# Eighteen stages on one core: the order of work around each stage boundary, the place of the last products, and the root of the norm

## The chip, the cores and the metric

The kernel runs on one core of one Trainium2 chip, as one program for the whole network. The metric is the device time of that program in microseconds, lower is better. The time before is the median of three runs, 3973.99 us (3971.36 to 3976.38).

## The reference

The input is one sequence of 256 tokens of 1024 features (tile 0 and tile 1 are its two halves of 128 tokens). Eighteen sublayers follow each other, and each has this form:

```
h = x * rsqrt(mean(x*x) + 1e-6) * gain           # (in stages 6 to 17 also * (1 + scale) + shift)
x = x + gate * sublayer(h)                       # gate only in stages 6 to 17, else 1
glu sublayer:  (silu(h @ w_gate) * (h @ w_up)) @ w_down
```

The kernel numbers them: 0 nsa attention, 1 moe, 2 ple, 3 moba attention, 4 moe, 5 ple, then 6 ffn, 7 rwkv, 8 ffn, 9 ffn, 10 mamba, 11 ffn, 12 ffn, 13 swa attention, 14 ffn, 15 ffn, 16 rwkv, 17 ffn. A moe stage computes all 32 experts and weighs them by the router. A ple stage multiplies a sigmoid of one product with another product. An ffn stage has 22 units of 128 hidden features, a moe stage 32.

## The kernel before

Each product of fp32 matrices is made of three: every weight piece of 128x1024 is split by ScalarE into a rounded high part (`split_hi`) and by VectorE, or for some pieces by GpSimd, into the rest (`split_lo_v`, `split_lo_g`), and the same holds for the activations. `mm3_tokens` issues the three matmuls (high x low, high x high, low x high). The split pieces live in eight slots; a piece can be split only once its slot's former piece has been used for the last time (`product["used", ...]`) and once its chunk has landed from DRAM in a ring of 12 units. Which slot a piece takes is written by hand, in the lists at the calls of `ffn`, `moe`, `ple` and in `swa` and `mamba`. Each engine follows a program in a fixed order, so that an instruction that waits holds back all that stand behind it on its engine. SyncE issues the weight chunks in order, and between them the gate rows (`load_gate`).

A glu stage (`plan_glu`, `glu_pe`, `glu_act`, `glu_dve`) goes over pairs of units. Step s = 2p + t is pair p for tile t: `gate_up(s)` is 24 matmuls of 512 columns, `silu(s)` and `up(s)` make the hidden features, `turn(s)` transposes them on TensorE, `high(s)` and `low(s)` split them, and `down(s, hf)` adds them (6 matmuls) to half hf of tile t's output. The steps overlap: `turn(s - 1)` stands inside `gate_up(s)` and the down products of step s - 2 behind it. `second(p)` plans the two pieces of the down weights of pair p.

A boundary is what lies between two stages. The output of tile t, half hf is added to x by `update(t, hf)` on VectorE (in stages 6 to 17 one scalar_tensor_tensor that multiplies by the gate row, line 238, then one add, line 226). Then the norm: `square_act` sums the squares on ScalarE, `var_dve` makes mean and half, `root_act` a first root by Ln and Exp on ScalarE (its table set loaded by `e.tables`, line 268), `root_dve` one Newton step and the scaling of half of the row (`unit_act` scales the other half), `pe` transposes the tile on TensorE, and `halves_act` and `halves_dve` apply gain and shift and split the result. TensorE's first product of the next stage waits for that (`x_lo`). `early(st + 1)` are the next stage's first weight pieces, which are split in this stretch too. In a glu stage tile 1 of the head is transposed by `second_tokens`, after k = 4 of the eight k of `gate_up(0)`. A mixer stage (attention, rwkv, mamba) transposes tile 1 before any product, because its products take both tiles.

The gate row of a stage is written from SBUF to DRAM and read back on all partitions; in the row that is read back, feature k*128 + p stands at p*8 + k, so that `gated_dve` reads it with a step of 8 elements.

## Time and profile before

| | |
|---|---|
| median of 3 runs | 3973.99 us |
| profiled execution, its own time | 3970.69 us |
| its span | 3968.9 us |
| TensorE busy | 3645.8 us (92%) |
| VectorE busy | 2628.6 us (66%) |
| ScalarE busy | 1798.6 us (45%) |
| GpSimd busy | 429.9 us (11%) |
| mean granted TensorE clock | 0.96 |

The span holds the instructions; the rest of the execution's own time, 1.8 us, lies around them. TensorE is idle for 323 us of the span. Each boundary can be seen in the timeline as a stretch of a few microseconds in which TensorE's rows carry an idle time in brackets, with the engine and line that ended it.

### The profile page before, as it was taken

How to read it: one execution, taken by the hardware profiler on the slowest of the kernel's cores; microseconds unless marked ns; L12 is line 12 of the kernel's file. 1: busy time of each engine (PE TensorE's matmuls, PEld its weight loads, DVE VectorE, ACT ScalarE, POOL GpSimd, SP SyncE). 2: the span in 40 equal slices, each digit the busy share in tenths (PEclk: the TensorE clock that was granted, in tenths of full speed). 3: DMA queues.
4: the chain of work that ended last, by engine and by line, in shares of the span. 5: the costliest groups of instructions: out<-in, count | busy, mean ns of one | idle time of the engine just before them, and what ended most of it. 6: DMA issues, size and time to landing. Idle time of an engine off the chain costs nothing.

```text
span 3968.9 us, 51736 instructions
## 1 busy us (share of the span) xinstructions
PE 3645.8 (92%) x19842; PEld 2996.3 (75%) x19842; DVE 2628.6 (66%) x4865; ACT 1798.6 (45%) x3151; POOL 429.9 (11%) x365
## 2 busy tenths in 40 slices
PE   6999998899898989889998998999989998899899
PEld 6767877688687867778787957878768787777677
DVE  4567765677576665577777677777667777665555
ACT  3254444544544433354546545454454544433343
POOL 2010002100001322200003410000000002322100
PEclk9899998999899999999999999999999999999999
DMA  5126852377485310167673416867347674300153
GB/s 229 54 81 244 281 196 81 122 282 282 144 292 212 108 43 1 38 218 285 224 276 128 165 65 220 294 226 272 122 139 288 221 290 154 117 12 1 59 181 106
DMA packets 170898, 670.13 MB, mean 169 GB/s; under 512 B 20512, under 2 KB 21024, under 8 KB 162464
## 3 DMA queue, kind: packets, MB, share of 16 engines
q1 hardware_dynamic: 170656, 666.83, 47.0%
q8 instruction: 160, 2.62, 0.3%
q14 instruction: 82, 0.67, 0.1%
HBM read 665.66 MB, written 1.10 MB: 168 GB/s over the span
## 4 chain that ended last, share of the span: by engine, by line
PE 77%; DVE 14%; ACT 7%; issue 2%; POOL 1%; DMA 0%; SPq 0%; DVEq 0%; ACTq 0%; POOLq 0%
PE pb L273 72%; PE pb L280 4%; ACT wp L264 2%; DVE wp L226 2%; DVE wk L238 2%; DVE wk L226 2%; DVE sq L238 1%; DVE pb L238 1%; ACT wk L264 1%; DVE xt L226 1%; ACT hT L264 1%; ACT sq L264 1%; ACT hx L264 1%; DVE hx L226 1%; ACT L264 1%
## 5 line engine op out<-in xcount | busy, mean ns | idle before, releaser
L273 PE MATMUL pb<-wp,hx 128*128 128x512 f32 (+1 forms) x6432 | 1587.7, 399 | 32.0 <-DVE hx L226 30.1
L226 DVE TENSOR_TENSOR wp<-ring,wp 128x1024 fp32r<-128x1024 f32 (+1 forms) x903 | 1057.9, 1205 | 608.1 <-ACT wp L264 607.3
L273 PEld LDWEIGHTS pb<-wp,hx 128*128 128x128 f32 x6432 | 1208.1, 192 | 283.9 <-DVE hx L226 22.6
L264 ACT ACTIVATE wp<-ring 128x1024 fp32r<-128x1024 f32 x936 | 957.7, 1053 | 401.4 <-PE pb L273 390.6
L273 PE MATMUL pb<-wp,ex 128*128 128x512 f32 x2928 | 702.0, 389 | 0.0
L273 PEld LDWEIGHTS pb<-wp,ex 128*128 128x128 f32 x2928 | 548.9, 188 | 113.6
L264 ACT ACTIVATE wk<-pb 128x256 f32<-128x256 f32 (+4 forms) x604 | 262.2, 439 | 624.5 <-PE pb L273 450.1
L226 POOL TENSOR_TENSOR wp<-ring,wp 128x512 fp32r<-128x512 f32 (+1 forms) x123 | 235.5, 1919 | 2692.6 <-ACT wp L264 2692.6
L273 PE MATMUL pb<-wk 128*128 128x128 f32 (+8 forms) x3008 | 388.5, 293 | 21.6 <-ACT wk L264 6.6
L273 PEld LDWEIGHTS pb<-wk 128*128 128x128 f32 (+4 forms) x3008 | 286.8, 172 | 115.1 <-issue 45.2
L273 PE MATMUL pb<-hx,wp 128*128 128x256 f32 x2688 | 344.3, 288 | 22.6 <-DVE hx L226 12.0
L273 PEld LDWEIGHTS pb<-hx,wp 128*128 128x128 f32 x2688 | 333.5, 195 | 30.7 <-issue 21.3
L243 DVE CUSTOM_DVE_ANT_0 ring<-ring,cact,prm 128x1024 f32<-128x1024 f32 x288 | 354.2, 1278 | 0.0
L264 ACT ACTIVATE ex<-pb 128x256 fp32r<-128x256 f32 x240 | 92.1, 385 | 514.9 <-PE pb L280 514.9
L280 PE MATMUL pb<-cst,wk 128*128 128x128 f32 (+2 forms) x1092 | 197.1, 284 | 64.6 <-DVE wk L226 48.5
L280 PEld LDWEIGHTS pb<-cst,wk 128*128 128x128 f32 (+2 forms) x1092 | 133.0, 142 | 125.0 <-DVE wk L226 56.6
L264 ACT ACTIVATE wk<-wk 128x256 f32<-128x256 f32 (+3 forms) x305 | 127.1, 435 | 185.7 <-DVE wk L238 65.6
L226 DVE TENSOR_TENSOR wk<-wk,pb 128x256 f32<-128x256 f32 (+1 forms) x256 | 117.5, 459 | 114.6 <-ACT wk L264 73.3
L280 PE MATMUL pb<-cst,sq 128*128 128x128 f32 x352 | 61.3, 326 | 135.0 <-DVE sq L232 128.1
L280 PEld LDWEIGHTS pb<-cst,sq 128*128 128x128 f32 x352 | 48.1, 167 | 149.2 <-issue 118.6
L226 DVE TENSOR_TENSOR ex<-pb,ex 128x256 fp32r<-128x256 f32 x240 | 100.7, 420 | 78.6 <-ACT ex L264 76.9
L226 DVE TENSOR_TENSOR wk<-pb,cst 128x256 f32<-128x256 f32 (+3 forms) x212 | 80.4, 429 | 73.5 <-PE pb L273 62.4
(176 smaller groups left out, 2767.7 us busy)
## 6 DMA issues: line engine op xcount, KB each, us to landing
ring<-weights SPq DMA_DIRECT2D x1088, 512.0 KB, 5.1
ring<-weights SPq DMA_DIRECT2D x35, 1536.0 KB, 6.5
ring<-weights SPq DMA_DIRECT2D x24, 1024.0 KB, 5.1
cst<-gate_rows SPq DMA_DIRECT2D x12, 512.0 KB, 4.3
cst<-consts SPq DMA_DIRECT2D x1, 1984.0 KB, 10.7
ring<-weights SPq DMA_DIRECT2D x1, 1280.0 KB, 5.4
ring<-weights SPq DMA_DIRECT2D x1, 1152.0 KB, 5.5
xt<-x_in SPq DMA_DIRECT2D x1, 1024.0 KB, 5.0
```

What stands on the lines that cost most here:

```text
L226: return self.real.tensor_tensor(out, a, b, op) if self.real else Uncounted()
L238: return self.real.scalar_tensor_tensor(out=out, in0=a, scalar=s, in1=b, op0=op0, op1=op1)
L243: return self.real.tensor_tensor_reduce(out=out, in0=a, in1=b, scale=1.0, scalar=first, op0=op0, op1=op1, accum_out=accum)
L264: return self.real.activation(out, a, func, bias=bias, scale=scale, accum_out=accum)
L273: return self.real.matmul(out, l, r, start=start, stop=stop, skip_group_check=skip)
L280: return self.real.transpose(out, a, self.identity[base:base + n, base:base + n])
```

## The change

1. **Root.** `root_act` goes, and with it the table load at the boundary. `var_dve` makes a first guess from the bits of the variance and `root_dve` takes three Newton steps, ten small VectorE instructions in all, each waiting for the one before.
2. **Gate row.** It is written to DRAM in the order of the features, element by element, and read with step 1 by `gated_dve`.
3. **Boundary.** The early pieces are now split one at a time between the other steps: one before the squares, one between them (VectorE: before `var_dve`), one before `halves`, the rest before tile 1's norm. Out of a glu stage VectorE does `halves_dve(0)` before `update(1, 0)`; the last step's `up` and `low` stand behind `var_dve(0)` and `root_dve(0)`, and its `silu` and `high` behind tile 0's squares.
4. **Last products.** The down weights of the last pair are split a step earlier, in slots that are free by then. Tile 0's last down products stand after k = 2 of the last `gate_up`, and the last four products are all tile 1's.
5. **Glu start.** Tile 1's head is transposed after k = 7, not 4. In ffn stages `turn(0)` stands after k = 5 of `gate_up(1)`, not 1.
6. **Slots.** Eight of the hand-written lists change.

```
@@ -745,8 +745,7 @@
...
             x, ps = X2[:, t, hf * 512:(hf + 1) * 512], pb[2 * t + hf][:, :]
-            p3 = ps.rearrange("p (k n) -> p k n", k=4)
-            e.stt(p3, p3, scale, gate_rows[:, hf * 4:(hf + 1) * 4, :], ALU.mult, ALU.mult).then_inc(
+            e.stt(ps, ps, scale, gate_row[:, hf * 512:(hf + 1) * 512], ALU.mult, ALU.mult).then_inc(
                 *v_step.up((st, "gated", t, hf)))
@@ -782,27 +781,24 @@
...
             e.wait_ge(*a_step[self.st, "square", t, 1])
-            v = self.column(t, 2)
-            e.ts(v, self.column(t, 0), self.column(t, 1), 1.0 / D, ALU.add, ALU.mult).then_inc(
-                *v_step.up((self.st, "var", t)))
-            e.wait_ge(*v_step[self.st, "var", t])
-            e.ts(self.column(t, 3), v, 1e-6, -0.5, ALU.add, ALU.mult).then_inc(*v_step.up((self.st, "half", t)))
-
-        def root_act(self, e, t):
-            e.wait_ge(*v_step["eps"])
-            e.wait_ge(*v_step[self.st, "var", t])
-            e.act(self.column(t, 4), self.column(t, 2), ACT.Ln, bias=eps[:, 0:1]).then_inc(*a_step.up((self.st, "log", t)))
-            e.wait_ge(*a_step[self.st, "log", t])
-            e.act(self.column(t, 5), self.column(t, 4), ACT.Exp, scale=-0.5).then_inc(*a_step.up((self.st, "root", t)))
+            v, h, y = self.column(t, 2), self.column(t, 3), self.column(t, 4)
+            e.ts(v, self.column(t, 0), self.column(t, 1), 1.0 / D, ALU.add, ALU.mult).then_inc(*v_step.up())
+            e.wait_ge(*v_step.last)
+            e.ts(h, v, 1e-6, -0.5, ALU.add, ALU.mult).then_inc(*v_step.up())
+            e.wait_ge(*v_step.last)
+            e.ts(v, h, -2.0, None, ALU.mult).then_inc(*v_step.up())
+            e.wait_ge(*v_step.last)
+            e.ts(y.bitcast(I32), v.bitcast(I32), -0.5, RSQRT_MAGIC, ALU.mult, ALU.add).then_inc(*v_step.up((self.st, "first", t)))
 
         def root_dve(self, e, t):
-            r = self.column(t, 5)
-            e.wait_ge(*a_step[self.st, "root", t])
-            e.wait_ge(*v_step[self.st, "half", t])
-            e.stt(self.column(t, 6), r, r, self.column(t, 3), ALU.mult, ALU.mult).then_inc(*v_step.up((self.st, "newton", t)))
-            e.wait_ge(*v_step[self.st, "newton", t])
-            e.ts(self.column(t, 7), self.column(t, 6), 1.5, r, ALU.add, ALU.mult).then_inc(*v_step.up((self.st, "r", t)))
-            e.wait_ge(*v_step[self.st, "r", t])
+            h, z = self.column(t, 3), self.column(t, 6)
+            e.wait_ge(*v_step[self.st, "first", t])
+            for y, r in ((4, 5), (5, 4), (4, 7)):
+                e.stt(z, self.column(t, y), self.column(t, y), h, ALU.mult, ALU.mult).then_inc(*v_step.up())
+                e.wait_ge(*v_step.last)
+                e.ts(self.column(t, r), z, 1.5, self.column(t, y), ALU.add, ALU.mult).then_inc(
+                    *v_step.up(*([(self.st, "r", t)] if r == 7 else [])))
+                e.wait_ge(*v_step.last)
             e.ts(XS[:, t, 0:512], X2[:, t, 0:512], self.column(t, 7), None, ALU.mult).then_inc(
@@ -893,49 +887,59 @@
...
 
-    def boundary_act(e, st, pieces=None, middle=()):
+    def boundary_act(e, st, first=None, then=None, middle=()):
         h, now = head_of(st + 1), early(st + 1)
-        split_hi(e, now[:2] if pieces is None else pieces)
+        split_hi(e, now[:2] if first is None else first)
+        then = now[2:] if then is None else then
+        if h is None:
+            for step in middle:
+                step()
+            return
+        h.square_act(e, 0, 0)
+        split_hi(e, then[:1])
+        h.square_act(e, 0, 1)
         for step in middle:
             step()
-        if h is None:
-            return
-        e.tables("natural_log_exp_and_others")
-        split_hi(e, now[2:3])
-        h.square_act(e, 0, 0)
-        split_hi(e, now[3:])
-        h.square_act(e, 0, 1)
-        h.root_act(e, 0)
         h.unit_act(e, 0)
-        h.square_act(e, 1, 0)
+        split_hi(e, then[1:2])
         h.halves_act(e, 0)
-        h.square_act(e, 1, 1)
-        h.root_act(e, 1)
+        split_hi(e, then[2:])
+        for hf in range(2):
+            h.square_act(e, 1, hf)
         h.unit_act(e, 1)
...
 
-    def boundary_dve(e, st, update, order, pieces=None, middle=()):
+    def boundary_dve(e, st, update, order, first=None, then=None, middle=()):
         h, now = head_of(st + 1), early(st + 1)
-        split_lo_v(e, now[:2] if pieces is None else pieces)
-        if h is not None:
-            h.gains_dve(e)
+        split_lo_v(e, now[:2] if first is None else first)
+        then = now[2:] if then is None else then
         before = order[:order.index((0, 1))]
...
             update(t, hf)
-        for step in middle:
-            step()
+        if h is not None:
+            h.gains_dve(e)
         update(0, 1)
         if h is not None:
-            split_lo_v(e, now[2:3])
+            split_lo_v(e, then[:1])
             h.var_dve(e, 0)
+            for step in middle[:1]:
+                step()
             h.root_dve(e, 0)
+            for step in middle[1:]:
+                step()
+            split_lo_v(e, then[1:2])
+        else:
+            for step in middle:
+                step()
+        if h is not None and middle:
+            h.halves_dve(e, 0)
         if (1, 0) not in before:
             update(1, 0)
-        if h is not None:
+        if h is not None and not middle:
             h.halves_dve(e, 0)
-            split_lo_v(e, now[3:])
         update(1, 1)
         if h is not None:
+            split_lo_v(e, then[2:])
             h.var_dve(e, 1)
@@ -1043,7 +1047,7 @@
...
         def second(p, by="v"):
-            at = [order[(4 * p + j) % 6 if p == P - 1 else 6 + j] for j in range(2)]
+            at = [order[(4 * P + j) % 6 if p == P - 1 else 6 + j] for j in range(2)]
             g.down.append([made(lambda I, j=j: unit(I, p)[1][:, j * 1024:(j + 1) * 1024], at[j], by) for j in range(2)])
@@ -1059,11 +1063,11 @@
...
             a = second(p - 1, by) if p and not late else []
-            b = gate_up(p + 1, 0, 2) if more else []
+            b = gate_up(p + 1, 0, 2) if more else second(p)
             g.split.append(a + b)
...
                 g.ada[2 * p + 1] = plan_ada()
-            a = second(p - 1) if late else second(p) if not more else []
+            a = second(p - 1) if late else []
             b = gate_up(p + 1, 2, 4, "g" if routed and p == 0 else "v") if more else []
@@ -1126,7 +1130,7 @@
...
 
-        second_tokens = {4: lambda: head.pe(e, 1)}
+        second_tokens = {7: lambda: head.pe(e, 1)}
         if g.routed:
@@ -1142,17 +1146,16 @@
...
             gate_up(0, second_tokens)
-            gate_up(1, {1: lambda: turn(0)})
+            gate_up(1, {5: lambda: turn(0)})
         for s in range(6 if g.routed else 2, last):
...
             whole_down(s - 2)
-        gate_up(last, {1: lambda: turn(last - 1)})
-        down(last - 1, 0)
+        turn(last - 1)
+        gate_up(last, {2: lambda: whole_down(last - 1)})
+        down(last - 2, 0)
         turn(last)
-        down(last - 1, 1)
-        for hf in range(2):
-            down(last - 2, hf)
-            down(last, hf)
+        down(last - 2, 1)
+        whole_down(last)
         boundary_pe(e, st)
@@ -1188,18 +1191,22 @@
...
             silu(5)
-        for s in range(6 if g.routed else 0, last + 1):
+        for s in range(6 if g.routed else 0, last):
             here = 1 if s % 2 == 0 and s else 0
...
             split_hi(e, g.split[s][here:])
-            if s == last - 1:
-                split_hi(e, early(st + 1)[:2])
             if g.ada.get(s) is not None:
...
             silu(s)
-        boundary_act(e, st, (), [lambda: high(last)])
+        high(last - 1)
+
+        def last_unit():
+            silu(last)
+            high(last)
+
+        boundary_act(e, st, early(st + 1)[:1], early(st + 1)[1:], [last_unit])
@@ -1255,17 +1262,17 @@
...
             modulations(5)
-        for s in range(6 if g.routed else 0, last + 1):
+        for s in range(6 if g.routed else 0, last):
             modulations(s)
...
             split_lo_v(e, g.split[s][here:])
-            if s == last - 1:
-                split_lo_v(e, early(st + 1)[:2])
             up(s)
-        boundary_dve(e, st, update, IN_TURN, (), [lambda: low(last)])
+        modulations(last)
+        low(last - 1)
+        boundary_dve(e, st, update, IN_TURN, early(st + 1)[:1], early(st + 1)[1:], [lambda: up(last), lambda: low(last)])
@@ -1781,7 +1788,7 @@
...
         W = lambda a, b: (lambda I: np.asarray(I["sw_w_qkv_2"])[0][:, a:b])
-        A = grouped(st, range(3, 8), W(1024, 1536), W(0, 1024), in_hx, "h", in_hx, "h", 3072,
+        A = grouped(st, (5, 6, 7, 3, 4), W(1024, 1536), W(0, 1024), in_hx, "h", in_hx, "h", 3072,
                     lambda I: np.asarray(I["sw_w_o_2"])[0], range(3, 8), 3, ("sw_q", "sw_k"), lambda h: C("swa"),
@@ -2045,7 +2052,7 @@
...
         c_dt = raw_chunk(128, 256, lambda I: ktiles(W(6144, 6176)(I)), (v_step, (st, "dt weights")))
-        w = Weights(st, [4, 5, 6, 7] * 8 + [4, 5] * 8, None,
+        w = Weights(st, [6, 7, 4, 5] * 8 + [4, 5] * 8, None,
                     (4096, D, lambda I, n0, n1: W(2048 + n0, 2048 + n1)(I)), (2048, D, lambda I, n0, n1: W(n0, n1)(I)),
@@ -3039,21 +3046,21 @@
...
     moe(1, 0, [0, 1, 2, 3, 4, 5, 6, 7], (x_lo, (0, "o", 7)))
-    ple(2, 0, [4, 5, 6, 7, 2, 3, 0, 1])
+    ple(2, 0, [0, 1, 2, 3, 6, 7, 4, 5])
     moba(3)
     moe(4, 1, [0, 1, 5, 4, 2, 3, 6, 7], (x_lo, (3, "o", 7)))
-    ple(5, 1, [2, 3, 5, 4, 6, 7, 0, 1])
-    ffn(6, 0, 0, 0, [5, 4, 6, 7, 0, 1, 2, 3])
+    ple(5, 1, [0, 1, 5, 4, 6, 7, 2, 3, 5, 4])
+    ffn(6, 0, 0, 0, [0, 1, 2, 3, 6, 7, 5, 4])
     rwkv(7, 0, 0)
-    ffn(8, 0, 2, 1, [4, 5, 6, 7, 3, 0, 1, 2], {i: (product, (7, "out", 1, 1)) for i in range(3)})
+    ffn(8, 0, 2, 1, [4, 5, 3, 0, 6, 7, 1, 2], {i: (product, (7, "out", 1, 1)) for i in range(3)})
     ffn(9, 1, 0, 0, [6, 7, 4, 5, 1, 2, 3, 0])
...
                                                 for i in range(8)})
-    ffn(12, 2, 0, 0, [5, 6, 3, 4, 1, 2, 7, 0])
+    ffn(12, 2, 0, 0, [7, 0, 3, 4, 5, 6, 1, 2])
     swa(13, 2)
-    ffn(14, 2, 2, 1, [6, 7, 0, 2, 1, 3, 4, 5], (x_lo, (13, "o", 7)))
-    ffn(15, 3, 0, 0, [0, 2, 6, 7, 4, 5, 1, 3])
+    ffn(14, 2, 2, 1, [1, 2, 6, 7, 0, 3, 4, 5], (x_lo, (13, "o", 7)))
+    ffn(15, 3, 0, 0, [0, 3, 1, 2, 6, 7, 4, 5])
     rwkv(16, 3, 1)
@@ -3115,7 +3122,7 @@
...
             a = l * 72 + s * 24 + 16
-            e.dma(d_gate[n].rearrange("(p k) -> p k", p=128), mods[:, a:a + 8]).then_inc(s_gate, 16)
+            e.dma(d_gate[n].rearrange("(k p) -> p k", p=128), mods[:, a:a + 8], True).then_inc(s_gate, 16)
             e.wait_ge(s_gate, 32 * n + 16)
```

Besides, `dma` takes the argument `by_element`, `first_head_act` loses its table load and `root_act`, and `Head` takes an argument that nothing reads.

## Rows read from the trace of the kernel before

**Rows 1.** Page, part 1: busy time, share of the span, instructions of each engine

```profile
PE 3645.8 (92%) x19842; PEld 2996.3 (75%) x19842; DVE 2628.6 (66%) x4865; ACT 1798.6 (45%) x3151; POOL 429.9 (11%) x365
```

**Rows 2.** Waits of TensorE, whole span: total us, times, longest us

```profile
PE pb L280 <- DVE sq L232: 128.1, 22, 24.0
```

**Rows 3.** Timeline, stage 14 to 15: start us, us, instruction, [idle before]

```profile
3120.91 7.07 PE L273 MATMUL pb<-wp,ex 128*128 128x512 f32 x30
...
3128.11 1.06 PE L280 MATMUL pb<-cst,sq 128*128 128x128 f32 x8
...
3132.10 5.30 PE L273 MATMUL pb<-wp,hx 128*128 128x512 f32 x15 [2.93 <-DVE hx L226]
...
3139.47 1.06 PE L280 MATMUL pb<-cst,sq 128*128 128x128 f32 x8 [2.06 <-DVE sq L232]
...
3141.86 0.41 DVE L226 TENSOR_TENSOR hx<-hT,hx 128x256 fp32r<-128x256 f32 x1
...
3145.07 1.28 ACT L264 ACT_TABLE_LOAD   x1
...
3147.26 0.69 PE L280 MATMUL pb<-cst,wk 128*128 128x128 f32 x2 [3.25 <-DVE wk L226]
```

**Rows 4.** Windows, stages 14 to 15 (two), 13 to 14; 0.57, 0.50: granted clock

```profile
3132.00:3136.00 4.00, 3.90 (x10) 3.09 (x11) 3.28 (x6) 1.31 (x4) 0.00 (x0) 0.57 0.01 2
3147.00:3152.00 5.00, 4.74 (x12) 3.79 (x13) 5.00 (x9) 2.39 (x3) 0.00 (x0) 0.50 0.92 288
2930.00:2937.00 7.00, 5.12 (x16) 4.07 (x16) 5.15 (x11) 3.48 (x10) 0.00 (x0) 0.50 0.12 40
```

**Rows 5.** Timeline, stage 14 to 15, the norm of tile 1 on VectorE

```profile
3137.52 0.40 DVE L233 TENSOR_SCALAR stat<-stat 128x1 f32<-128x1 f32 x2 [0.79 <-ACT sq L264]
...
3138.59 0.21 DVE L233 TENSOR_SCALAR stat<-stat 128x1 f32<-128x1 f32 x1
3138.84 0.49 DVE L232 TENSOR_SCALAR sq<-xt,stat 128x512 f32<-128x512 f32 x1
```

**Rows 6.** Groups by shape, VectorE, whole span: busy us, mean ns, idle before

```profile
L238 DVE SCALAR_TENSOR_TENSOR pb<-pb,cst 128x512 f32<-128x512 f32 x48 | 53.7, 1120 | 4.7 <-PE pb L273 4.7
L226 DVE TENSOR_TENSOR xt<-xt,pb 128x512 f32<-128x512 f32 x64 | 43.7, 686 | 11.5 <-PE pb L273 9.9
L238 DVE SCALAR_TENSOR_TENSOR wk<-wk,prm,pb 128x256 f32<-128x256 f32 x64 | 28.6, 477 | 8.9 <-PE pb L273 8.9
```

**Rows 7.** Timeline, mixer to ffn: into stage 14 (two rows), into 11

```profile
2920.12 1.23 DVE L226 TENSOR_TENSOR wp<-ring,wp 128x1024 fp32r<-128x1024 f32 x1 [5.57 <-ACT wp L264]
...
2929.83 1.94 PE L280 MATMUL pb<-cst,sq 128*128 128x128 f32 x8 [6.76 <-DVE sq L232]
...
2400.93 1.11 PE L280 MATMUL pb<-cst,sq 128*128 128x128 f32 x8 [4.17 <-DVE sq L232]
```

**Rows 8.** Timeline, ffn to mixer: into stage 7 (two rows), 10, 16

```profile
1272.39 1.06 ACT L264 ACTIVATE wp<-ring 128x1024 fp32r<-128x1024 f32 x1 [5.14 <-PE pb L273]
...
1284.59 1.94 PE L280 MATMUL pb<-cst,sq 128*128 128x128 f32 x8 [5.84 <-DVE sq L232]
...
2111.77 1.94 PE L280 MATMUL pb<-cst,sq 128*128 128x128 f32 x8 [9.09 <-DVE sq L232]
...
3335.42 1.94 PE L280 MATMUL pb<-cst,sq 128*128 128x128 f32 x8 [6.22 <-DVE sq L232]
```

**Rows 9.** Timeline, stage 1 to 2 (moe to ple, two rows), and start of stage 1

```profile
564.73 1.27 PE L280 MATMUL pb<-cst,sq 128*128 128x128 f32 x8 [3.89 <-DVE sq L232]
...
569.04 7.23 PE L273 MATMUL pb<-wp,hx 128*128 128x512 f32 x24 [3.04 <-DVE hx L226]
...
310.17 1.08 PE L280 MATMUL pb<-cst,wk 128*128 128x128 f32 x4 [5.57 <-DVE wk L232]
```

**Rows 10.** DMA issues: count, KB each, median us from issue to landing

```profile
ring<-weights SPq DMA_DIRECT2D x1088, 512.0 KB, 5.1
...
gate_rows<-mods SPq DMA_DIRECT2D x12, 4.0 KB, 5.4
```

More of the change, by code:

```diff
@@ L280, in tp, with dma @@
         return self.real.transpose(out, a, self.identity[base:base + n, base:base + n])
-    def dma(self, out, a):
-        return self.real.dma_start(out, a) if self.real else Uncounted()
+    def dma(self, out, a, by_element=False):
+        return self.real.dma_start(out, a, allow_slow_non_contiguous=by_element) if self.real else Uncounted()
 class Chunk:
@@ L734, in added_dve @@
         return update
-    gates, gate_rows = [], gate_row.rearrange("q (p k) -> q k p", k=8)
+    gates = []
     def plan_gate(st, l, s):
@@ L756, in build_program, with __init__ @@
     class Head:
-        def __init__(self, st, outs, ada=None):
-            self.st, self.outs, self.ada = st, outs, ada
+        def __init__(self, st, outs, ada=None, gated_units=False):
+            self.st, self.outs, self.ada, self.gated_units = st, outs, ada, gated_units
         def gain(self, n, k):
@@ L884, in first_head_act @@
                 h.square_act(e, t, hf)
-            h.root_act(e, t)
             h.unit_act(e, t)
@@ L894, in first_head_dve @@
             h.halves_dve(e, t)
-    def boundary_act(e, st, pieces=None, middle=()):
+    def boundary_act(e, st, first=None, then=None, middle=()):
         h, now = head_of(st + 1), early(st + 1)
-        split_hi(e, now[:2] if pieces is None else pieces)
+        split_hi(e, now[:2] if first is None else first)
[7 more added lines that the diff above has]
+        h.square_act(e, 0, 1)
         for step in middle:
             step()
-        if h is None:
-            return
-        e.tables("natural_log_exp_and_others")
-        split_hi(e, now[2:3])
-        h.square_act(e, 0, 0)
-        split_hi(e, now[3:])
-        h.square_act(e, 0, 1)
-        h.root_act(e, 0)
         h.unit_act(e, 0)
-        h.square_act(e, 1, 0)
+        split_hi(e, then[1:2])
         h.halves_act(e, 0)
-        h.square_act(e, 1, 1)
-        h.root_act(e, 1)
+        split_hi(e, then[2:])
+        for hf in range(2):
+            h.square_act(e, 1, hf)
         h.unit_act(e, 1)
         h.halves_act(e, 1)
-    def boundary_dve(e, st, update, order, pieces=None, middle=()):
+    def boundary_dve(e, st, update, order, first=None, then=None, middle=()):
         h, now = head_of(st + 1), early(st + 1)
-        split_lo_v(e, now[:2] if pieces is None else pieces)
-        if h is not None:
-            h.gains_dve(e)
+        split_lo_v(e, now[:2] if first is None else first)
+        then = now[2:] if then is None else then
         before = order[:order.index((0, 1))]
@@ L1917, in ffn @@
         S = stage(st)
-        S.head = Head(st, [("h", None, Hh, Hl)], (l, s))
+        S.head = Head(st, [("h", None, Hh, Hl)], (l, s), True)
         def unit(I, p):
```

## The prediction

> **What bounds the kernel now.** The page's first part comes first: TensorE is busy for 3645.8 of 3968.9 us [rows 1], so only its 323 us of idle time and its slow stretches can be won or lost. The waits of TensorE say where they lie: 128.1 us, the largest item, end when VectorE has scaled a row for the transposes of the norm [rows 2]. That is a boundary matter, so the timeline of each kind of boundary is read next, and one of the three from ffn to ffn stands in full [rows 3]: TensorE waits 2.93 us between tile 0's transposes and the first product, 2.06 us for tile 1's transposes and 3.25 us at `turn(0)`, 8.24 us together. The windows add what such gaps cost afterwards: behind the first gap TensorE was granted 0.57 of its clock and did 10 products in 3.90 us busy, behind the third 0.50 and 12 in 4.74 us [rows 4]; at full clock (0.50 is 1.2 of 2.4 GHz) 30 products take 7.07 us [rows 3], 0.236 us each, so 10 and 12 would be 2.4 and 2.8 us. The half clock cost 1.5 and 1.9 us, 3.4 us a boundary.
>
> **Unit prices.** *Norm.* Tile 1's norm now takes from 3137.52 to 3138.84, 1.3 us, Ln and Exp included; two VectorE steps that wait for each other are 0.25 us apart [rows 5]. Ten such steps are 2.5 us: the new root is 1.2 us longer, once a tile. The bits step is not in these rows; it is taken as one more of them. *Update.* The gate multiply takes 1.12 us, an add of the same width 0.69, a multiply of that form at half the width, step 1, 0.48 [rows 6]. So step 1 lies between 0.69 and 1.12 us; taken is 0.75, nearer to the row of the same width (twice 0.48 is 0.95). An update falls from 1.8 to 1.4 us. *Halves.* From the transposes' start to the end of the first split pair is 2.8 us with VectorE and ScalarE free [rows 3], so 1.75 us idle behind the 1.06 us of transposes; three more subtractions of 0.41 end the tile at about 4.1. *Piece.* 1.06 us on ScalarE [rows 8], then 1.23 on VectorE [rows 7]. *Table load.* 1.28 us on ScalarE [rows 3].
>
> **Ffn to ffn (3 boundaries).** After tile 0's last product TensorE now has 15 + 6 + 6 + 12 = 39 products instead of 24, 9.2 us instead of 5.7: the transposes of tile 0 don't wait. But `low(last)` stands behind the root. From that product VectorE needs about 0.7 us (rest of the first update, gains), 1.4 (update), 1.2 (piece), 1.0 (four steps), 0.4 (`up`), 1.5 (six steps), 0.5 (scaling), 0.4 (`low`) = 7.1, and TensorE asks after 27 products, 6.4: 0.6 us idle. Then 1.75 idle. `gate_up(0)` follows whole, 5.7 us; from the start of the transposes TensorE is through at 1.06 + 1.75 + 5.7 = 8.5. VectorE: 4.1 (halves) + 2.8 (both updates of tile 1, now behind them) + 1.2 (piece, over the squares) + 2.5 + 0.5 = 11.1. So 2.6 us idle, and now 1.75 behind tile 1's transposes too, which nine products covered. `turn(0)` comes 18 products into `gate_up(1)`, 2.8 + 4.2 = 7.0 us after those transposes; VectorE has halves 4.1, two pieces and `up` done at about 8.1: 1.1 us idle. The sum is 0.6 + 1.75 + 2.6 + 1.75 + 1.1 = 7.8 us for 8.24. With only one half-clock stretch left of two (1.5 us; the gaps are shorter, the two around tile 1's transposes are together longest) it is 9.3 for 11.6: **-2.3 each, -6.9**. The missing table load before `silu(0)` gives only 0.3 us of this, as the two pieces on VectorE end last. The Trainium skill (ScalarE: Activation LUTs, What ACT_TABLE_LOAD costs) puts a switch at 2.66 us, drain included; the trace has 1.28 and no such pause. By the page the saving would be 1.6 us, these three -3.9 more.
>
> **Mixer to ffn.** Into stage 14 the first pieces are held 5.57 us by slots 6 and 7 of the stage's own out-weights, and the updates stand behind them; TensorE waits 6.76 [rows 7]. In slots 1 and 2 nothing holds them: two updates are done before tile 0's last product, and behind it 1.4 + 1.2 + 2.5 + 0.6 = 5.7 us lie beside 24 products. So 6.8 is gone; a piece that now stands before the halves costs 1.2, tile 1 1.4 more, `turn(0)` 1.8 less (1.4 for 3.2): -6.0, and of 4.0 us of half clock (5.12 us busy at 0.50 [rows 4], half of it, and the stretch at `turn(0)`) 1.5 stays: **-8.5**. Into 8 and 17 the same hold remains (slots 4 and 5 stay first): three updates save 1.1, the root takes 1.2, the piece 0.4, tile 1 1.1, `turn(0)` gives 1.9 and its clock 1.5: **-1.8 each**. Into 11 no piece holds (4.17 us [rows 7]), one update saves 0.4: +0.8, +1.2, +0.9, -1.9, -1.5 and a little of the clock: **-1.0**. Together -13.1.
>
> **Mixer to moe (2).** Tile 0 is +0.9 (the piece). Router logits of tile 1 come 2.9 us later, being behind all of `gate_up(0)` and the transposes; all of the choice is on VectorE and TensorE already waits 5.57 us for its end [rows 9]. With `silu(0)` behind the later halves **+3.8 each, +7.6**.
>
> **Ffn to mixer (4).** Both tiles are wanted before a product. Into 10 and 13: 9.09 us idle [rows 8]; `low` +0.6, updates of tile 1 -0.8, `update(1, 0)` no longer beside the transposes +0.3, the root +1.2: **+1.2 each**. Into 16 VectorE has no split to do, so `update(1, 0)` was wholly hidden and is not now: 6.22 us [rows 8] become 8.7, **+2.5**. Into 7 the same, but there ScalarE's third piece waited 5.14 us for a slot [rows 8] and the new list frees it: **-2.6**. Together +2.3. In the mixers the first Exp or Ln now needs a table load; where TensorE runs behind, it is at no cost, if bare 1.28 x 4 = 5 us.
>
> **Moe to ple (2).** Into 2: 3.89 us [rows 9] were a held slot too, now 0.7; 3.04 and 2.8 stay near 2.9 (ple waits for the whole tile); 24 products took 7.23 us for 5.7: **-4.7**. Into 5 no hold: **+0.4**. **Ple onward (2).** Into 3 the root twice, +2.4; into 6 +1.2 + 0.4 + 0.8 - 1.9 = +0.5: **+2.9**. **The end.** Two shorter updates: **-0.7**.
>
> **Gate rows (12).** 128 runs of 32 bytes become 1024 of 4. The trace has 5.4 us to landing [rows 10] and SyncE waits for it. Between nothing and eightfold (43 us) I take the low end, since 512 KB in long runs land in 5.1 us [rows 10]: the 5.4 are hardly a matter of size. Cover: the ring's 12 units; a pair of an ffn uses 9 units in 72 products, 17 us, so 22 us of work are ahead.
>
> **Sum.** -6.9 - 13.1 + 7.6 + 2.3 - 4.3 + 2.9 - 0.7 = -12.2 us on the profiled execution's 3970.7, 3958.5. The median of the runs lies 3.3 us above that execution: **3962 us**.
>
> **Rivals.** (1) *The clock stays up.* The long gaps are cut, and no half-clock stretch is left in the nine glu starts where I keep 1.5 us: -13, 3949. For it: the 2.06 us gap has none behind it [rows 3]; against: 2.6 + 1.75 around 1.06 busy. (2) *The gate multiply is no cheaper.* Then two updates of 0.37 a boundary on the path come back in 12 stages, +9: 3971. Against it: both rows with step 1 [rows 6]. (3) *`turn(0)` waits as before,* since `silu(0)` and `up(0)` stand behind halves that are later: +1.9 in nine stages, 17: 3979. (4) *Slower: a piece in the norm's chain.* Before, one piece stood ahead of tile 0's norm; now VectorE has a piece ahead of each of `var_dve(0)`, `halves_dve(0)` and tile 1's norm, and each waits for ScalarE's copy, which waits for a slot or a chunk. If one is late by its own 1.06 + 1.23 = 2.3 us at all 17 boundaries: +39, 4001. For it: 5.57 and 5.14 us of such holds; against: the new lists follow the order in which slots come free. It decides from 1.2 us a boundary (20 us). (5) *Slower: the element-wise gate rows.* At 43 us to landing, 21 us beyond the ring's cover, 12 times: +250, 4210; it decides from 24 us. The Trainium skill speaks for it (DMA: Bandwidth & Descriptors, Rules for kernel authors): a strided last dimension becomes one descriptor per element, and should be rearranged. No row here shows a transfer of that form.
>
> **Chances.** Forecast 0.38 (own range 3952 to 3971), rival 1 0.20, 2 0.10, 3 0.12, 4 0.14, 5 0.06. 0.2% is 8 us, about what a measurement of this kernel can tell: faster is below 3966. The forecast gives 0.30 to faster and 0.08 to same, rival 1 0.20 to faster, rival 2 0.03 and 0.07, rival 3 same, 4 and 5 slower: 0.53, 0.27, 0.20. The range reaches from rival 1's side, 3940, to half of rival 4, 3988.
>
> **What the profile after would show.** No wait before tile 0's transposes out of ffn stages and into 14; about 0.6 us before the last down products; ten steps on `stat`, 2.5 us, in place of 1.3; the gate multiply at 0.75 us; 2.6 us before tile 1's transposes and 1.75 behind; about 1.1 to 1.4 at `turn(0)`; moe's 5.57 near 9; no more than a few us more to the gate row's landing. Wrong would make it: many more or fewer half-clock stretches, or ScalarE copies that wait for TensorE between the steps of the norm.

## The result, and the profile after

The changed kernel takes 3983.28 us, median of 20 runs (3974.58 to 3989.84), the kernel before in runs beside it 3976.25 (3968.33 to 3980.76). The ratio is 1.0019, 95% interval 1.0012 to 1.0025: slower by 7.5 us, where -12 us was forecast. It lies in the range, on the other side of no change.

Part 1 of the page, as [rows 1]:

```profile
PE 3661.6 (92%) x19842; PEld 3006.9 (75%) x19842; DVE 2637.7 (66%) x5081; ACT 1758.3 (44%) x3061; POOL 431.2 (11%) x365
```

The span is 3987.2 us, so TensorE is idle for 325.6 us, 2.5 more than before. It is busy 15.8 us longer, with as many instructions: the same products ran slower. From here on *half-clock work* is the time in which TensorE was busy while it was granted 0.5 of its clock, summed over the trace: 220.5 us before, 247.4 after. Half of it is time lost: between the two profiles of the changed kernel that stand below it differs by 21.5 us and TensorE's busy time by 12.0. The largest wait fell as it should, and another grew (waits of TensorE, as [rows 2]; the `hx` wait was 45.4 us in 20 times before):

```profile
PE pb L280 <- DVE sq L232: 116.8, 15, 25.0
PE pb L273 <- DVE hx L226: 62.7, 30, 4.0
```

TensorE's timeline from stage 14 to 15 stands against [rows 3]:

```profile
3141.93 3.04 PE L273 MATMUL pb<-wp,ex 128*128 128x512 f32 x12 [0.20 <-DVE ex L226]
3144.81 1.03 PE L280 MATMUL pb<-cst,sq 128*128 128x128 f32 x8
3147.72 7.32 PE L273 MATMUL pb<-wp,hx 128*128 128x512 f32 x24 [1.88 <-DVE hx L226]
3155.65 1.07 PE L280 MATMUL pb<-cst,sq 128*128 128x128 f32 x8 [0.61 <-DVE sq L232]
3158.51 5.94 PE L273 MATMUL pb<-wp,hx 128*128 128x512 f32 x18 [1.79 <-DVE hx L226]
3164.28 0.38 PE L280 MATMUL pb<-cst,wk 128*128 128x128 f32 x2
...
3169.71 0.41 PE L280 MATMUL pb<-cst,wk 128*128 128x128 f32 x2 [2.29 <-DVE wk L226]
```

The last products and tile 0's transposes go through almost without a wait, as planned. Then 24 products take 7.32 us where 5.7 is full clock, and 18 take 5.94 for 4.24: two slow stretches, not one. `turn(0)` (3164.28) no longer waits, but `turn(1)` (3169.71) does, 2.29 us. In the kernel before it did not:

```profile
3155.58 0.38 PE L280 MATMUL pb<-cst,wk 128*128 128x128 f32 x2
```

What VectorE does meanwhile (same stretch; `mods` is the modulations of the first pair, lines between them left out):

```profile
3160.31 2.36 DVE L226 TENSOR_TENSOR wp<-ring,wp 128x1024 fp32r<-128x1024 f32 x2 [0.47 <-ACT wp L264]
3162.59 0.42 DVE L226 TENSOR_TENSOR wk<-wk,pb 128x256 f32<-128x256 f32 x1
3162.92 1.28 DVE L243 CUSTOM_DVE_ANT_0 ring<-ring,cact,prm 128x1024 f32<-128x1024 f32 x1
...
3166.54 0.42 DVE L226 TENSOR_TENSOR ex<-pb,ex 128x256 fp32r<-128x256 f32 x1
3166.88 2.35 DVE L226 TENSOR_TENSOR wp<-ring,wp 128x1024 fp32r<-128x1024 f32 x2
3169.14 0.42 DVE L226 TENSOR_TENSOR wk<-wk,pb 128x256 f32<-128x256 f32 x1
```

Two pieces, `up(0)`, three modulations of 1.28 us, `low(0)`, two pieces and `up(1)` stand in one queue with no gap behind its first piece: `turn(1)` waits for its end. The gate multiply, as [rows 6], takes 0.695 us:

```profile
L238 DVE SCALAR_TENSOR_TENSOR pb<-pb,cst 128x512 f32<-128x512 f32 x48 | 33.4, 695 | 17.7 <-PE pb L273 17.7
```

And the gate row's issues, as [rows 10]:

```profile
gate_rows<-mods SPq DMA_DIRECT2D x12, 4.0 KB, 10.4
```

### The profile page after: what moved, and what is told of

It reads as the page before. It is cut to its first block, busy times and chain, and to the rows that moved or that the text cites. A ratio compares the mean times of both kernels' runs of the same rounds, so it can differ in the third digit from the quotient of the medians.

```text
span 3987.2 us, 51832 instructions
## 1 busy us (share of the span) xinstructions
PE 3661.6 (92%) x19842; PEld 3006.9 (75%) x19842; DVE 2637.7 (66%) x5081; ACT 1758.3 (44%) x3061; POOL 431.2 (11%) x365
## 2 busy tenths in 40 slices
DMA packets 181650, 670.13 MB, mean 168 GB/s; under 512 B 31264, under 2 KB 31776, under 8 KB 173216
## 4 chain that ended last, share of the span: by engine, by line
PE 77%; DVE 14%; ACT 6%; issue 2%; POOL 1%; DMA 0%; SPq 0%; DVEq 0%; ACTq 0%; POOLq 0%
PE pb L273 73%; PE pb L280 4%; DVE wp L226 3%; ACT wp L264 3%; DVE wk L238 2%; DVE wk L226 2%; DVE sq L238 1%; ACT wk L264 1%; DVE stat L233 1%; ACT hT L264 1%; ACT hx L264 1%; DVE ring L243 1%; DVE xt L226 1%; DVE hx L226 1%; DVE sq L226 1%
## 5 line engine op out<-in xcount | busy, mean ns | idle before, releaser
L273 PE MATMUL pb<-hx,wp 128*128 128x256 f32 x2688 | 341.7, 288 | 21.9 <-DVE hx L226 12.1
```

The lines of the kernel that those rows point to most:

```text
L273: return self.real.matmul(out, l, r, start=start, stop=stop, skip_group_check=skip)
```

## The experiments

All ratios are to the kernel before, run on the same chip; 0.001 is 4 us. *Idle* is TensorE's, and it and *half-clock work* are of one profiled execution each. In the kernels with `fill` in their name and in e_last TensorE has added products, which count as busy, so their idle time can't be compared with the others'.

| kernel | ratio (95%) | idle us | half-clock work us |
|---|---|---|---|
| before, two profiles | 1 | 323.1, 322.5 | 220.5, 228.0 |
| changed, two profiles | 1.0019 (1.0012 to 1.0025) | 325.6, 325.1 | 247.4, 225.9 |
| a_root | 1.0065 (1.0052 to 1.0079) | 349.7 | 225.4 |
| a_gate | 0.9961 (0.9948 to 0.9973) | 311.3 | 221.9 |
| a_order | 0.9968 (0.9956 to 0.9981) | 312.9 | 234.9 |
| a_start | 1.0026 (1.0017 to 1.0035) | 323.7 | 248.9 |
| b_root | 0.9988 (0.9979 to 0.9997) | 311.1 | 242.7 |
| b_start | 1.0002 (0.9993 to 1.0011) | 316.8 | 229.4 |
| b_tile1 | 1.0006 (0.9997 to 1.0015) | 319.4 | 236.8 |
| c_best | 0.9957 (0.9945 to 0.9970) | 308.2 | 231.2 |
| d_fill_after | 1.0018 (1.0009 to 1.0027) | 304.8 | 206.9 |
| d_fill_best | 0.9919 (0.9905 to 0.9932) | 271.2 | 181.5 |
| e_mod_before | 0.9994 (0.9984 to 1.0003) | 317.9 | 230.0 |
| e_mod_after | 0.9985 (0.9975 to 0.9994) | 317.9 | 224.9 |
| e_mod_fill_after | 0.9957 (0.9940 to 0.9974) | 292.2 | 183.0 |
| e_mod_fill_best | 0.9919 (0.9903 to 0.9934) | 268.8 | 184.3 |
| e_mod_start | 0.9989 (0.9980 to 0.9997) | 314.6 | 241.9 |
| e_last | 0.9917 (0.9903 to 0.9931) | 274.7 | 188.8 |

### One part alone, on the kernel before

**a_root**: `var_dve` and `root_dve` of the change, no `root_act`, no table load at the boundary.

> The kernel before with one part of the change: the norm's root by VectorE alone (ten dependent steps, no Ln and Exp, no table load at the boundary). Theory A (the root costs what was priced, 1.2 us more a tile, on the path for tile 1 at all 17 boundaries and for tile 0 at about nine, with up to 1.3 us back at turn(0) in eleven glu starts): +15 to +30 us, ratio 1.004 to 1.0075. Theory B (the removed table loads and ScalarE steps give the same back, and the loss comes from the order of the glu starts): within 5 us, ratio 0.999 to 1.0013.

Measured 1.0065, +26 us: theory A. The timeline of its boundary into stage 3, where both tiles are wanted before a product, has 10.11 and 10.17 us where the kernel before has 9.10 and 9.03. Tile 1, here and then in the kernel before:

```profile
628.66 1.97 PE L280 MATMUL pb<-cst,sq 128*128 128x128 f32 x8 [10.17 <-DVE sq L232]
```

```profile
622.09 1.97 PE L280 MATMUL pb<-cst,sq 128*128 128x128 f32 x8 [9.03 <-DVE sq L232]
```

That is 1.0 and 1.1 us a tile. In the whole kernel it is idle time: +26.6 us. The table load it saves gives little: from tile 1's transposes to `turn(0)` into stage 15 are 7.4 us here, 7.8 before.

**a_gate**: the gate row by element, read with step 1.

```
-            e.stt(p3, p3, scale, gate_rows[:, hf * 4:(hf + 1) * 4, :], ALU.mult, ALU.mult)
+            e.stt(ps, ps, scale, gate_row[:, hf * 512:(hf + 1) * 512], ALU.mult, ALU.mult)
```

> The kernel before with one part of the change: the gate row stored by element so that the gate multiply reads it with step 1. Theory A (the multiply falls from 1.12 to 0.69 us, and about two such multiplies a boundary lie on the path in 12 stages): -8 to -12 us, ratio 0.997 to 0.998. Theory B (what the shorter multiply gives is taken back by a later landing of the gate row or by slower work behind the gaps): within 3 us, ratio 0.9993 to 1.0007.

Measured 0.9961, -15.5 us: theory A, and a little more than its 8 to 12 us. Idle time fell by 11.8 us. The row's first transfer takes 11.1 us to land in this run for 5.4 before. SyncE waits longer for it, 127.6 us in 12 times for 60.1; none of TensorE's or VectorE's waits ends with it.

**a_order**: the boundary's order, the last products and the slot lists; root, gate row and starts as before. The old root comes back into the new order like this (one place of the edit to the changed kernel):

```
         for step in middle:
             step()
+        e.tables("natural_log_exp_and_others")
         h.root_act(e, 0)
         h.unit_act(e, 0)
```

> The kernel before with the boundary's order, the slot lists and the last products of the change, and nothing else of it (root, gate row and glu starts as before; the root stands behind the last silu and high, and needs its tables loaded once more there). Theory A (this part gains what the idle time shows: the held pieces into 2, 7 and 14 are gone, 3.8 + 2.6 + 6.8 us, and nothing is lost elsewhere): -10 to -20 us, ratio 0.995 to 0.9975. Theory B (what it saves comes back in other places: more half clock, ex and hx waited for in the last step and behind the pieces): within 6 us, ratio 0.9985 to 1.0015.

Measured 0.9968, -12.7 us, idle -10.2: theory A in size. Its "nothing is lost elsewhere" does not hold: from stage 9 to 10 this part alone has 3.1 us more idle time (see *Held pieces* below). (The lists can't be tried without the order: the early pieces of the old order would wait for slots that come free only behind them.)

**a_start**: the starts alone.

```
-        second_tokens = {4: lambda: head.pe(e, 1)}
+        second_tokens = {7: lambda: head.pe(e, 1)}
-            gate_up(1, {1: lambda: turn(0)})
+            gate_up(1, {5: lambda: turn(0)})
```

> The kernel before with the two glu starts of the change alone: tile 1's transposes behind all of gate_up(0), turn(0) after five blocks of gate_up(1). Theory A (the starts lose by themselves what the first undo gave, 6.5 us: nothing covers the wait behind tile 1's transposes, 1.75 us in eleven starts, less the 1.4 us that turn(0) saves): +4 to +12 us, ratio 1.001 to 1.003. Theory B (they lose only behind the slower root and the later tile 1 of the changed kernel): -6 to +2 us, ratio 0.9985 to 1.0005.

Measured 1.0026, +10.3 us: theory A's size, but not its reason. The idle time is nearly the same, 323.7 us; half-clock work is up 28 us in this profile (21 us above the second one of the kernel before). Into stage 15 of this kernel:

```profile
3160.62 4.40 PE L273 MATMUL pb<-wp,hx 128*128 128x512 f32 x18 [1.79 <-DVE hx L226]
...
3172.19 0.41 PE L280 MATMUL pb<-cst,wk 128*128 128x128 f32 x2 [3.45 <-DVE wk L226]
```

Here the 18 products ran at full clock, and the time went into a wait of 3.45 us at `turn(1)`. So TensorE is early or slow, and `turn(1)` comes at the same time either way, counted from tile 1's transposes: 14.4 us here, 14.1 in the changed kernel.

The four parts alone sum to +25.8 - 15.5 - 12.7 + 10.3 = +7.9 us, against 7.5 for the whole change. That they meet so well is luck, as the next runs show: together the two losing parts cost less than 36.1 us, and the two winning ones give less than 28.2.

### One part taken back in the changed kernel

> The changed kernel with the root as before: Ln and Exp on ScalarE behind a table load, in glu stages behind the last silu and high, and low(last) ahead of the root on VectorE. Theory A (the root is the loss): -15 to -30 us against the changed kernel outside the ffn-to-ffn boundaries, where the second table load takes 1 to 3 us back: ratio to before 0.994 to 0.998. Theory B (the starts are the loss): the table loads (1.28 us each, twice a boundary) come back onto the path as the ten steps leave it, within 5 us of the changed kernel, ratio 1.0005 to 1.003.

> The changed kernel with its glu starts put back: tile 1's transposes after four of the eight feature blocks of gate_up(0) and turn(0) after one of gate_up(1). Theory A (the root is the loss): the idle time only changes places, within 3 us of the changed kernel's 3983, ratio to before 1.001 to 1.0027. Theory B (the starts are the loss, because the first 24 products run together at half clock and nothing covers the wait behind tile 1's transposes): 10 to 20 us faster than the changed kernel, ratio 0.9968 to 0.9994, with 20 us or more of TensorE's 247 us of half-clock work gone.

> The changed kernel with one of the two glu starts put back: tile 1's transposes after four blocks of gate_up(0), turn(0) stays after five of gate_up(1). Theory A (the place of tile 1's transposes is the loss, and turn(0)'s move a gain of up to 1.4 us a start): faster than with both put back, ratio 0.998 to 1.000. Theory B (turn(0)'s move is a loss too, or nothing): ratio 1.000 to 1.001, the same as with both put back or slower.

**b_root** measured 0.9988: the new root costs 12 us there, half of its 26 alone. One reason may be that the old root needs its tables a second time behind the last `silu` in that order; no run tests it by itself. Theory A had the direction, not the size. **b_start** measured 1.0002, 7 us less than the changed kernel: theory B's direction, below its size. **b_tile1**, 1.0006, can't be told from it: the place of tile 1's transposes is most of the starts' loss there, and no gain from `turn(0)`'s move is seen.

> Order, slot lists, last products and gate row of the change, with the root and the glu starts as before: both parts that lost by themselves are left out. Theory A (the parts add up: gate row -14, order and slots -9 as the changed kernel has them): about -20 us, ratio 0.994 to 0.996. Theory B (the second table load in each glu stage, and the order, take back what the gate row gives): -6 to -12 us, ratio 0.997 to 0.9985, and the gate row alone (0.9961) stays the fastest.

**c_best** measured 0.9957, -17 us, inside theory A's range; but the parts don't add up as it says: alone they give 15.5 and 12.7 us. It is not below the gate row alone (0.9961) by more than can be told.

### Is the loss the clock?

Products on constants, as the kernel has them elsewhere, fill the waits of the starts (`repeated_pe`, computing nothing that is used). They stand in the eight ffn starts; the expectations count nine, but the ple stages do not run this code:

```
             ps = bk.hold(e, 4 + s % 3, key, (v_out, key))
+            repeated_pe(e, ps, ahead)
```

> The changed kernel with ten short products on constants (0.156 us each in its profile, 1.6 us) put into the 1.9 us that TensorE waits behind tile 0's transposes and ten into the wait behind tile 1's, in the nine ffn and ple starts. They compute nothing that is used. Theory A (the waits of the starts are what makes the clock fall, and the half-clock work behind them is what the change lost): the half-clock work of TensorE falls by 20 us or more of 247, 8 to 20 us faster than the changed kernel, ratio to before 0.997 to 1.000. Theory B (the half clock comes from elsewhere or by chance): within 4 us of the changed kernel, ratio 1.001 to 1.003.

> Order, slots, last products and gate row of the change with the root and starts of the kernel before, and besides ten short products on constants behind tile 0's transposes and sixteen (2.5 of 3.3 us) before turn(0) in the nine ffn and ple starts. Theory A (the clock follows the waits): -8 to -20 us against the same kernel without them (0.9957), ratio 0.991 to 0.994. Theory B (the clock isn't theirs to keep): ratio 0.995 to 0.997.

> The changed kernel once more, for a second profile. Theory A (the 27 us more of half-clock work are the change's own): half-clock work again 240 to 255 us. Theory B (a good part is chance of one execution, as its 3987 us span lies 4 us above the median): half-clock work 225 to 240 us and a span near 3980.

> The kernel before once more, for a second profile. Theory A: half-clock work again 215 to 225 us, span within 3 us of 3972. Theory B (chance): 225 to 240 us, span above 3973.

**d_fill_best** measured 0.9919, 15 us below c_best: theory A. **d_fill_after** measured 1.0018: nothing, although half-clock work fell by 19 us or more. Ten of the added products take 2.4 us in the trace, not 1.6 as its expectation has it, and what follows them starts 0.1 to 0.2 us later. That is 2 to 3 us in eight starts, too little to explain the missing gain. Its trace into stage 15:

```profile
3151.19 1.07 PE L280 MATMUL pb<-cst,sq 128*128 128x128 f32 x8 [1.14 <-DVE sq L232]
...
3154.25 4.35 PE L273 MATMUL pb<-wp,hx 128*128 128x512 f32 x18
...
3165.24 0.41 PE L280 MATMUL pb<-cst,wk 128*128 128x128 f32 x2 [3.43 <-DVE wk L226]
```

The products behind both waits now run at full clock, and `turn(1)` waits 3.43 us instead of 2.29. From tile 0's transposes to `turn(1)` are 24.9 us in both kernels. The clock was not what bounded this stretch.

**after_2** and **before_2** show what a profile can tell. At equal idle time (325.6 and 325.1) the changed kernel's spans are 3987.2 and 3974.7 us, half-clock work 247.4 and 225.9, most of the difference in stages 1 and 4. So the 27 us between the first two profiles were in good part chance; the means, 236.7 and 224.3, differ by 12.4 us, 6.2 us of time. Both half-clock figures lie in theory B's range (chance); the spans do not follow it, 3974.7 us lying 5 us below its 3980 and 3970.6 in theory A's range. Idle time hardly varies and the medians differ by 7 us, so of the loss some 2.5 us are idle time and the rest, 4.5 to 5 us, is slower work.

### Is it VectorE?

The modulations of the first pair (3.8 us of VectorE) move from step 1 to step 10 of each ffn stage. Seven stages have them in step 1, not eight as the expectation says: in stage 17 none are left.

```
+            if not routed and P > 6 and p == 5:
+                g.ada[2 * p] = plan_ada()
...
-            if (p < 10) if not routed else (2 <= p <= 14):
+            if ((0 if P <= 6 else 1) <= p < 10) if not routed else (2 <= p <= 14):
```

> The changed kernel with the three modulation products of VectorE (1.28 us each) that stand in step 1 of each ffn stage moved to step 10 of the same stage, in all eight ffn stages; their weights are loaded later too. Theory V (VectorE bounds the start: its 31.6 to 33 us of work up to the third turn fill that stretch): up to 3.8 us a start less, against what TensorE needs at its clock then, together -8 to -24 us against the changed kernel, ratio to before 0.996 to 1.000. Theory C (TensorE's clock bounds it): within 4 us of the changed kernel, ratio 1.001 to 1.003.

> The kernel before with the same move of the modulations. Theory V: VectorE's 30.4 to 31.5 us lie 2 to 3 us below its stretch of 33 to 35 us there, so less is won than in the changed kernel: -3 to -12 us, ratio 0.997 to 0.9992. Theory C: within 3 us, ratio 0.9993 to 1.0007.

> The changed kernel with both: the modulations moved, and the ten and ten short products in the waits. Theory V: now the clock that the products keep up isn't taken back by VectorE, and they pay as with the old root: 8 us or more below the run with the modulations moved alone, ratio to before 0.993 to 0.997. Theory C (the added products are no gain in this order of the starts, for they are themselves as long as the waits): within 4 us of the run with the modulations moved alone.

> The fastest so far (order, slots, gate row; root and starts as before; added products; 0.9919) with the modulations moved. Theory V: another -8 to -20 us, ratio 0.987 to 0.990. Theory C: within 3 us, 0.991 to 0.9927.

> The kernel before with the two glu starts of the change and the modulations of the first pair moved to step 10. Theory V (the starts alone lose 10 us, ratio 1.0026, because turn(0), pieces and modulations then queue on VectorE up to the third turn): with the modulations away the starts cost 3 us or less against the same kernel with the old starts (0.9994), ratio 0.998 to 1.0003. Theory C (the gaps and the half clock behind them are the loss, whatever VectorE has to do): the starts cost 8 us or more again, ratio 1.0014 to 1.0025.

> The changed kernel with the root as before (tables loaded again behind the last silu and high), the modulations moved, and the ten and ten short products in the waits. Theory V (the parts add: the same with the new root is 0.9957, the root 0.0031 of it in the changed kernel): -10 to -16 us against that run, ratio 0.9915 to 0.9932. Rival (the new root costs less once VectorE has room): within 5 us of it, 0.9945 to 0.997.

**e_mod_after** measured 0.9985, 13.5 us below the changed kernel; **e_mod_before** 0.9994, 2.4 us, not to be told from nothing. The same edit pays after the change and hardly before it. **e_mod_fill_after**, 0.9957: with the modulations away the added products are worth 11 us, where they were worth nothing. **e_mod_start**, 0.9989: the starts, which cost 10 us alone, now cost nothing against the same kernel with the old starts (0.9994). Three of the four are theory V's; e_mod_before lies in theory C's range (0.9993 to 1.0007), just outside theory V's. **e_mod_fill_best**, 0.9919, gives nothing more, as in theory C's range: in the kernel that it is made from, d_fill_best, `turn(1)` waits 0.6 us at most in the ffn starts, so there was little to win, which theory V did not expect. The windows show the same from tile 1's transposes to `turn(1)`, into stage 15 (length, then busy us of TensorE, its weight loads, VectorE, ScalarE, GpSimd; clock). First the changed kernel:

```profile
3155.60:3169.70 14.10, 9.97 (x40) 7.76 (x41) 12.18 (x22) 8.76 (x17) 0.00 (x0) 0.88 0.49 153
```

then e_mod_after:

```profile
3139.00:3151.10 12.10, 8.66 (x40) 6.50 (x40) 8.71 (x16) 8.74 (x17) 0.00 (x0) 1.00 0.32 96
```

VectorE is busy for 12.18 of 14.10 us, then for 8.71 of 12.10; TensorE does the same 40 instructions. The two windows also differ in clock (0.88 and 1.00), but that alone shortens nothing: d_fill_after has full clock there and needs 14.05 us. The other stages say the same. In the seven ffn starts with modulations this stretch takes 14.0 to 14.5 us in the changed kernel (both profiles), in a_start and in d_fill_after, whatever the clock; in e_mod_after it takes 12.1 to 13.3, and in stage 17 of the changed kernel, which has no modulations, 13.3.

**e_last**, old root, new starts, modulations moved, added products: 0.9917, 3942.15 us, 32 us (0.8%) faster than the kernel before, as expected by theory V. With d_fill_best (3943.02) and e_mod_fill_best (3942.56) it is the fastest here; the three can't be told apart, and all beat the kernel before and the changed one.

## Why the prediction was wrong

**The step that failed** is "With only one half-clock stretch left of two (1.5 us; the gaps are shorter, the two around tile 1's transposes are together longest) it is 9.3 for 11.6", and its like in the other starts. The terms for the clock were 5.7 (three ffn to ffn), 2.5 (into 14), 3.0 (8 and 17), 2.0 (11) and 1.5 (2): 14.7 us to be won. The rest of the sum, the idle time, was then +2.5 us. Measured: idle +2.5 and +2.6 us in two pairs of profiles, and half-clock work +12.4 us on the mean of two profiles each, 6.2 us lost where 14.7 was to be won (4.5 to 5 by the medians, see after_2). These 21 us are the error: forecast and measurement are 19.7 us apart (-12.2 and +7.5).

**Where it lies.** The time between the same two TensorE products, one in the middle of each stage, gives each boundary a measured change (means of two profiles each), here with its forecast behind it. Ffn to ffn, three together: -2.7 us for -6.9. Into 8, 17, 11 and 14: +2.2 for -1.8, -0.6 for -1.8, +3.5 for -1.0, -6.5 for -8.5. Into 10: +4.5 for +1.2. Into 7, 13 and 16, where no clock term stood: -3.0 for -2.6, +0.9 for +1.2, +1.9 for +2.5. In the stretches that the clock terms stand for, half-clock work rose from 77.8 to 82.2 us, 2.2 us lost for 14.7 won; the other 4 us lie elsewhere in the trace. Stage 15, shown above, is not where the time went: from tile 0's transposes to `turn(2)`, the same work, the three starts behind an ffn stage got 3.4 us shorter together and the five others 6.6 us longer.

That the idle time came out at the forecast +2.5 us is luck: moe stages got 3.3 us of it for 7.6, and two things were missing or too low. One is the kernel's own first norm, whose two roots stand in no sum: TensorE waits 25.02 and 6.07 us there for 23.97 and 5.11, +2.0. The other is stage 10, +3.5 idle for +1.2.

**Why it failed.** Shown: both gaps still have slow products behind them (7.32 and 5.94 us), and what bounds a start of the changed kernel is VectorE's queue up to `turn(1)`. The working followed that queue to `turn(0)` and stopped there; it said that a stall goes, and did not ask what is late next. Behind `turn(0)` stand 3.8 us of modulations, `low(0)`, two pieces and `up(1)`, all later by the longer root, by both updates before tile 1's norm and by tile 1's later transposes. Where TensorE is faster it waits for them (3.43 us). Open is how much of the starts' 10 us is this queue by itself and how much slow products behind it: with the modulations moved the starts cost nothing, because they then save idle time (314.6 us in e_mod_start, 317.9 in e_mod_before), while half-clock work is still higher (241.9 and 230.0). The price of the slow stretches before the change was low as well: the windows of [rows 4] end at 3136 and 3152 us, while the timeline has 5.30 us for the 15 products of [rows 3] and 8.14 us for the 24 behind `turn(0)`, 1.8 and 2.5 us over full clock for the 1.5 and 1.9 read there.

**The root** was priced nearly right: ten steps from 3138.53 to 3141.06 in the timeline, 2.5 us, and 1.0 to 1.1 us more a tile where nothing hides it, for 1.2. As a part it is the largest, +26 us alone. **The gate multiply** measured 0.695 us, at the lower bound, for 0.75; alone -15.5 us where rival 2 put it at 9, so rival 2 is out. **The element-wise rows** land after 10.4 us, 5 more than taken, with no wait of TensorE for them; rival 5 is out. The Trainium skill's rule (DMA: Bandwidth & Descriptors, Rules for kernel authors), one descriptor per element, agrees with the trace: packets under 512 B rose from 20512 to 31264, which is 12 times 1024 less 128. Its cost, 5 us a row, is hidden.

**Held pieces.** Into 14 the wait of 6.76 us is gone, as said; into 2 tile 0's 3.89 us too. The order as a part gave 12.7 us. Rival 4, a piece in the norm's chain, was to lose 39: as a loss at all boundaries it is out. Into stage 10 its mechanism is there, and nearly the last sign that the prediction named for being wrong: a ScalarE copy that waits for TensorE, here just ahead of the norm's squares.

```profile
2110.25 1.06 ACT L264 ACTIVATE wp<-ring 128x1024 fp32r<-128x1024 f32 x1 [6.44 <-PE pb L273]
...
2115.40 0.44 PE L280 MATMUL pb<-cst,wk 128*128 128x128 f32 x2 [2.46 <-DVE wk L226]
```

The first square, whose input VectorE has ready at 2108.28 us, starts behind that copy at 2111.22, and the last `silu` behind both squares, so that the last `turn` waits 2.46 us. That wait is in no sum; a_order has it too, 2.09 us.

**Ffn to ffn.** Idle 0.2, 1.88, 0.61, 1.79 and 0 at `turn(0)` for 0.6, 1.75, 2.6, 1.75 and 1.1: the third was small because the 24 products before it ran slowly (7.32 us for 5.7), and 2.29 us at `turn(1)` were in no sum. **Moe.** The waits before the router's logits grew by 2.1 us (1.64 to 3.78 into stage 1), and the wait for the choice did not grow: its two times are 11.2 us in the second profile of before and 11.4 in the second of after. So "5.57 near 9" is wrong and +3.8 each was too much. **Ffn to mixer.** Into 16 a wait of 7.81 us was measured for [rows 8]'s 6.22, +1.6 for +2.5.

**Rivals.** Rival 1, the clock stays up, is out: the gaps keep it down, and d_fill_after shows that it would not have paid by itself. Rival 3, `turn(0)` waits as before because `up(0)` is late (3979 us), came nearest in time; its mechanism is right one step later, at `turn(1)`. The Trainium skill's 2.66 us per table switch (ScalarE: Activation LUTs, What ACT_TABLE_LOAD costs) would by the estimate of the prediction have made a_root's starts shorter by 1.6 us; `turn(0)` moved by 0.4, and all 22 table loads of the kernel before take 1.28 us.

## What to carry to other kernels

Follow the queue of the second-busiest engine through the whole stretch that an edit touches, not only to the wait that it removes: here the wait went from `turn(0)` to `turn(1)`, and what TensorE won in clock it waited away. An edit that puts work on an engine that is last (ten small steps for Ln and Exp) can cost more than all the waits that a better order takes away; try the parts alone before they are bundled, since here two of four lost 36 us and two won 28, and do not count on their sum: the two winners together gave 17. And where products slow down behind a short wait, products on constants inside the wait can be worth 15 us, but only if no other engine is due there.

## What the runs showed of the hardware

- A multiply of VectorE on 128x512 whose second operand is read with step 8 (32 bytes apart) takes 1.12 us, with step 1 0.695, about the same as an add (0.687).
- A 4 KB store of 1024 single elements lands after 10.4 us, of 128 runs of 32 bytes after 5.4: far from eightfold.
- Dependent steps on VectorE of one column (128x1) begin 0.25 us apart, the first guess in integer form 0.19 us after the step that it waits for: ten are 2.5 us, for 1.3 us of the six before, Ln and Exp on ScalarE included (the norm of tile 1 into stage 15).
- Two executions of one kernel, with idle time equal to 0.5 us, differ by 21.5 us in half-clock work and by 12.5 us in span: a single profile can't price an edit that acts on the clock by so little. The Trainium skill (TensorE: Matmul & The Clock Gate, Part 1: The HAM clock gate) says that the number of slow products of one kernel varies with the run; the trace agrees.
- Keeping TensorE busy in eight starts (26 short products each) lowered half-clock work by 50 us in the profile (c_best 231.2, d_fill_best 181.5), of which 31 lie in the starts, from tile 0's transposes to `turn(2)`; why the rest fell elsewhere is open.
